# Where the TensorE operands start in SBUF: moving tiles to multiples of 2048 bytes, weight buffers to 64 past a multiple of 128

## What is computed

```python
# block 1
u = rms_norm(x) @ w_in                      # 1024 -> sparse attention, RWKV and merge columns
y = g0 * (o_nsa @ proj_nsa) + g1 * (o_rwkv @ proj_rwkv)
x = x + y @ w_out                           # 1024 -> 1024
x = x + (silu(a) * b) @ ffn_down            # a, b = split(conv(rms_norm(x) @ ffn_up)), inner width 2816
# block 2
x = x + 0.5 * norm(swiglu(norm(x)))         # 1024 -> 2816 (twice) -> 1024
x = x + norm((sig(g_a) * (att @ w_att) + sig(g_m) * (ml @ w_mlstm)) @ w_out_2)
x = x + 0.5 * norm(swiglu(norm(x)))         # the same shapes again
```

## Time and profile before

| | |
|---|---|
| median of 3 runs | 2446.37 us (2446.28 to 2447.52) |
| the profiled execution, first to last instruction | 2445.3 us |
| what lies around the span (median less span) | 1.1 us |
| instructions | 38,821, of which 13,906 matmuls and as many weight loads |
| mean granted TensorE clock | 0.990 |
| HBM traffic | 200.76 MB read, 2.10 MB written |

### The profile page before, as it was taken

One profiled execution on the slowest core, in us unless ns is written; L12 is line 12 of the kernel. 1 busy time (PEld: TensorE's weight loads), 2 busy tenths in 40 slices (PEclk: granted clock), 3 DMA queues, 4 the chain that ended last, 5 costly groups with the idle time before them and its releaser, 6 DMA issues.

```text
span 2445.3 us, 38821 instructions
## 1 busy us (share of the span) xinstructions
PE 2395.1 (98%) x13906; PEld 1956.1 (80%) x13906; DVE 1065.3 (44%) x1843; ACT 935.3 (38%) x1278; POOL 1033.9 (42%) x754
## 2 busy tenths in 40 slices
PE   8999998899999999999999999999999999999999
PEld 6878777777888888888888877887888878888886
DVE  4466475455555522222222855763333448222212
ACT  3345432243555522444423322224434624444322
POOL 4222230035455554555544533443343355555554
PEclk9999999999999999999999899999999998999999
DMA  5211110022222233232233222222222222322232
GB/s 158 70 44 44 61 62 4 3 96 98 90 94 96 100 105 101 89 98 98 95 103 105 98 69 72 84 79 69 78 77 84 71 95 69 100 97 94 95 102 95
DMA packets 60732, 204.21 MB, mean 84 GB/s; under 512 B 10940, under 2 KB 11708, under 8 KB 60380
## 3 DMA queue, kind: packets, MB, share of 16 engines
q1 hardware_dynamic: 55152, 196.45, 24.3%
q10 hardware_dynamic: 5488, 6.44, 0.9%
HBM read 200.76 MB, written 2.10 MB: 83 GB/s over the span
## 4 chain that ended last, share of the span: by engine, by line
PE 89%; DVE 8%; issue 2%; ACT 1%; DMA 0%; SPq 0%; DVEq 0%; ACTq 0%
PE psum L400 86%; DVE rope_t L2537 2%; DVE qk_st L2536 1%; PE psum L647 1%; DVE rope_t L2529 1%; DVE qk_st L2539 1%; PE psum L1087 0%; DVE inv L2154 0%; PE psum L473 0%; PE psum L467 0%; ACT dd L1434 0%; DVE tmp L2455 0%; DVE a_t L2095 0%; PE psum L769 0%; DVE zm L1796 0%
## 5 line engine op out<-in xcount | busy, mean ns | idle before, releaser
L373 POOL TENSOR_TENSOR w_lo<-raw,w_hi 128x512 fp32r<-128x512 f32 x732 | 1005.9, 1396 | 1391.0 <-ACT w_hi L1240 1391.0
L400 PE MATMUL psum<-h_hi,w_hi 128*128 128x512 f32 x2128 | 852.9, 401 | 13.2 <-DVE h_lo L1830 10.0
L400 PE MATMUL psum<-h_lo,w_hi 128*128 128x512 f32 x2128 | 835.6, 393 | 0.0
L1240 ACT ACTIVATE w_hi<-raw 128x1024 fp32r<-128x1024 f32 x366 | 385.9, 1055 | 696.7 <-PE psum L400 681.5
L400 PE MATMUL psum<-h_hi,w_lo 128*128 128x512 f32 x2128 | 535.2, 390 | 0.0
L400 PEld LDWEIGHTS psum<-h_hi,w_hi 128*128 128x128 f32 x2128 | 403.9, 190 | 110.4 <-issue 26.0
L400 PEld LDWEIGHTS psum<-h_lo,w_hi 128*128 128x128 f32 x2128 | 403.9, 190 | 84.0 <-issue 3.2
L400 PEld LDWEIGHTS psum<-h_hi,w_lo 128*128 128x128 f32 x2128 | 399.0, 188 | 83.8 <-issue 0.5
L1796 DVE TENSOR_TENSOR tmp<-psum,rst 128x512 f32<-128x512 f32 x100 | 69.1, 691 | 322.4 <-PE psum L400 322.2
L400 PE MATMUL psum<-hid_hi,w_hi 128*128 128x512 f32 x528 | 208.0, 394 | 0.0
L400 PE MATMUL psum<-hid_lo,w_hi 128*128 128x512 f32 x528 | 208.0, 394 | 0.0
(11 more groups left out here) (427 smaller groups left out, 2615.3 us busy)
## 6 DMA issues: line engine op xcount, KB each, us to landing
raw<-in_w SPq DMA_DIRECT2D x366, 512.0 KB, 3.3
x<-in_x SPq DMA_DIRECT2D x4, 512.0 KB, 6.4
x<-in_x ACTq DMA_DIRECT2D x1, 2048.0 KB, 8.9
out_y<-x SPq DMA_DIRECT2D x8, 256.0 KB, 2.3
mask<-in_mask ACTq DMA_DIRECT2D x1, 1536.0 KB
tmp<-in_cmp_w ACTq DMA_DIRECT2D x2, 512.0 KB, 6.0
masks<-in_masks ACTq DMA_DIRECT2D x1, 768.0 KB, 4.8
lora<-in_lora ACTq DMA_DIRECT2D x1, 512.0 KB, 3.5
```

The lines of the kernel that those rows point to most:

```text
L373: pool.tensor_tensor(w_lo[:, g.slot, part], raw[:, g.slot, part], w_hi[:, g.slot, part].bitcast(F32), ALU.subtract).then_inc(sem("lo_ready ...
L400: return pe.matmul(out, lhsT, rhs, start=start, stop=stop)
L1240: act.activation(w_hi[:, g.slot], raw[:, g.slot], ACT.Copy).then_inc(sem("hi_ready"), 1)
```

## The change

Tiles are declared in another order, and four dead tiles are put in as padding. No instruction is added, removed or moved on any engine; only addresses differ.

```diff
-        raw = sb("raw", [128, 2, 1024])
-        w_hi = sb("w_hi", [128, 2, 1024], F32R)
-        w_lo = sb("w_lo", [128, 2, 1024], F32R)
-        x = sb("x", [128, KD, T])
-        h_hi = sb("h_hi", [128, KD, T], F32R)
-        h_lo = sb("h_lo", [128, KD, T], F32R)
-        tmp = sb("tmp", [128, 8, T])
         par = sb("par", [128, NPAR])
...
-        rst = sb("rst", [128, T])
...
         moment = sb("moment", [128, 2, TB])
+        sb("page_pad", [128, 304])
+        x = sb("x", [128, KD, T])
+        h_hi = sb("h_hi", [128, KD, T], F32R)
+        h_lo = sb("h_lo", [128, KD, T], F32R)
+        tmp = sb("tmp", [128, 8, T])
+        rst = sb("rst", [128, T])
+        raw = sb("raw", [128, 2, 1024])
+        sb("w_pad", [128, 16])
+        w_hi = sb("w_hi", [128, 2, 1024], F32R)
+        w_lo = sb("w_lo", [128, 2, 1024], F32R)
...
         ys = ExitStack()
+        sb("y_pad", [128, 440], scope=ys)
         y_hi = sb("y_hi", [128, KD, T], F32R, scope=ys)
...
         gap = sb("gap", [128, 5, T], scope=ffn)
+        sb("hid_pad", [128, 496], scope=ffn)
         hid_hi = sb("hid_hi", [128, KF, T], F32R, scope=ffn)
...
         par_if = sb("par_if", [4, 2], scope=z2)
+        sb("att_pad", [128, 232], scope=z2)
         att = ExitStack()
```

## The result

The changed kernel takes 2481.4 us (median of 4 runs, 2479.0 to 2481.6) against 2446.9 us (2446.3 to 2449.1): a ratio of 1.0134, with a 95% interval of 1.0120 to 1.0149. It is 34.4 us slower. The forecast was 14 us faster, and the range ended at 2452.

A forecast was written before the change was run, and what follows sets the result against it. TensorE's matmul pace was taken as the bound. Gains for hid 10.5, y 2.9 and ah 0.6 us, everything else zero, took the 2445.3 us span to 2431.3, plus 1.1 for the median: 2432.4 us; range 2345 to 2452.

The forecast's parts named there:

- What bounds the kernel: Whole kernel: the end is set by how fast matmuls follow each other; TensorE holds 89% of the chain of waits.
- the semaphore waits: Waits ahead of each k, one of two explanations for hid's slower pace than h; rejected in favour of operand place.
- the pricing of the place: Moving tiles: hid, y, ah gain 14.0 us from h's remainder over 128; h's move and shifted weights cost zero.
- The evidence that tipped it: Output product and last h matmul: without a load beside them no shorter (397 against 398 ns), so shifted weights cost zero.
- The sum for hid, y and ah: Moving tiles reaching 226.7 ns: hid 10.5 us, y 2.9, ah 0.6, together 14.0 us gained.
- The rival of the match: All matmul streams: fast only if moving operand and weights agree modulo 128; h loses 42.5 us, total 2488.6 us; chance 0.20.
- VectorE and the others: Tiles of VectorE, ScalarE, GpSimd and DMA: new places priced at zero; 1% of VectorE's chain share would be 2 us.
- The rule of the Trainium skill: SBUF reads: 16-byte lines, two hits each; all tiles but pj_in already start on one, so nothing would change.

The follow-up runs named there:

- apart3: Weights and h at multiples of 2048 as in w0, first-block y at distance 192, second 0; first three matmuls of each output unit set apart; 2450.8 us.
- w0: The changed kernel without its 64-byte w_pad, so both weight buffers return to multiples of 2048; 2431.7 us, 0.9939 of the kernel before.

## Why the prediction was wrong

- **What bounds the kernel** held: TensorE's pace, by matmul, set the end, and nearly all of it came through (35.2 us more of TensorE's busy time, 34.5 of span). That the place of the operands sets the pace, and not the semaphore waits, held too.
- **The step that failed** is the pricing of the place: the moving tile's remainder over 128 was taken as what counts, and the 64 bytes of the weights as nothing. Of the five placements on show before, one was fast, and it was at once the only multiple of 128 and the only match with the weights; the prediction said so, and still put the match at 0.20. What counts is the distance between moving tile and weights modulo 256. The change set h, hid, y and ah to 192, where hid had been before, and so h lost 6.0 ns a matmul.
- **The evidence that tipped it** was the last matmul of a stream, without a load beside it. Its length was read rightly, and the step from it failed: it took it that the place of the weights can matter only through a load that runs beside the matmul. The same matmul, as much without a load beside it, takes 397 ns at distance 192 and 388 at 0 (the pair of lines under apart3), so it had the harm in it already. What was wanted was a stream over other weights, and no row had one.
- **The sum for hid, y and ah** was right under its condition: with the weights matching, w0 gained 15 us where 14.0 were worked out, and hid alone 12.7 us where its part was 10.5, within its interval.
- **The rival of the match** had mechanism and sign, with 128 bytes where 256 count: 2488.6 us against 2481.4 measured. Its price for h, 6384 x 6.66 = 42.5 us, was too high: 226.7 ns is the settled pace, and with the unsettled matmuls after each pause h before had 227.3 ns on average (after: 233.3), 6.0 ns x 6176 = 37 us. The 2 us that are left lie within the spread of the runs.
- **VectorE and the others** kept their times, as priced: the operation of the earlier trace rows took

```profile
L1801 DVE TENSOR_TENSOR tmp<-psum,rst 128x512 f32<-128x512 f32 x100 | 69.0, 690 | 337.5 <-PE psum L405 337.3 <-DVE rst L2455 0.2
```

- **The rule of the Trainium skill** ("SBUF — State Buffer", section "Specifications (TRN2)") on lines of 16 bytes, of which a stream wants two hits each, would have had no change at all. All tiles but pj_in start on such a line in the kernel before, in the changed one and in w0, and these three take 2447, 2481 and 2432 us: it isn't the rule that decides here.

## What to carry to other kernels

When one-pass fp32r matmuls with a fresh load each stream back to back at full clock, compare the starts of moving tiles and weights: place them a multiple of 256 bytes apart (here both lay at multiples of 128), and check the pace by the distance of two equal units in the timeline. Alignment of either operand by itself is the wrong question; 64 bytes ahead of the weights cost 50 us here, more than the whole layout can gain (15 us). One line of 64 bytes of padding ahead of hid_hi gave most of that gain, and when a trace offers two explanations that always occur together, a chance of 0.20 for the unwelcome one is too low.

## What was not expected of the hardware

The pace depends on where two tiles lie relative to each other, counted modulo 256 bytes: 226.7 ns at distance 0, 229 to 236 at all others tried. It is a property of the stream, not of the matmul, with a settled state that is reached some matmuls after a pause and then mostly kept, and it vanishes at half the clock. The harm shows on a matmul without a load beside it, too. Why zero is the fast distance, and whether a phase or the load of a matmul's own weights beside the one before carries it, stays open.
